# Sparse attention of the prompt: who weights and sums the index dots

## What is computed

```python
def indexer_scores(iq, iw, ik):
    dots = jax.nn.relu(jnp.einsum('bqhd,bsd->bqhs', iq, ik).astype(F32))
    return jnp.einsum('bqhs,bqh->bqs', dots, iw.astype(F32))

# for each block of 128 queries
sc = indexer_scores(iqb, iwb, ik)                 # 8 index heads
sc = jnp.where((key_pos[None, :] <= t[:, None])[None], sc, -jnp.inf)
_, idx = lax.top_k(sc, kk)                        # kk = 256
# softmax attention of 8 heads over the selected keys alone
```

## Time and profile before

| | us |
|---|---|
| median of 3 runs | 4081.56 (4080.29 to 4085.12) |
| the profiled execution | 4081.96 |
| its span, first to last instruction | 4079.6 |
| TensorE busy | 3440.1 (84%) |
| VectorE busy | 1736.2 (43%) |
| ScalarE busy | 1046.0 (26%) |
| GpSimd busy | 293.9 (7%) |

### The profile page before, as it was taken

How to read it: one execution, slowest core, us unless ns; L and a number is a source line. 1 busy time by engine, 2 the same in 40 slices (tenths; PEclk the granted TensorE clock), 3 DMA queues, 4 the chain that set the end, 5 groups by cost and what they waited for, 6 DMA issues and landing times. The chain is left out here.

```text
span 4079.6 us, 54190 instructions
## 1 busy us (share of the span) xinstructions
PE 3440.1 (84%) x20745; PEld 2868.6 (70%) x20771; DVE 1736.2 (43%) x2979; ACT 1046.0 (26%) x2049; POOL 293.9 (7%) x386
## 2 busy tenths in 40 slices
PE   8998849317568887889999999798599899999998
PEld 8986632105234444469999999797366699999997
DVE  2136611782378777521111256443244311112566
ACT  2134511001222222221111244321144311111444
POOL 0001122202000000000000000233000000000002
PEclk8997855558768877789999999898699899999999
DMA  3110122202300000011111211121200111112121
GB/s 98 43 41 21 31 73 58 62 6 63 118 16 19 19 18 11 11 50 43 46 41 46 89 40 51 43 46 64 79 29 27 47 46 41 46 41 80 51 59 45
DMA packets 235295, 189.81 MB, mean 47 GB/s; under 512 B 53473, under 2 KB 214258, under 8 KB 235090
## 3 DMA queue, kind: packets, MB, share of 16 engines
q1 hardware_dynamic: 227458, 169.84, 13.8%
q0 software_dynamic: 7664, 17.58, 1.4%
HBM read 158.11 MB, written 31.12 MB: 46 GB/s over the span
## 5 line engine op out<-in xcount | busy, mean ns | idle before, releaser
L1730 PE MATMUL ffn1u_ps<-h_hi,ffn1u_whi 128*128 128x384 f32 (+1 forms) x1056 | 348.1, 330 | 10.0 <-DVE h_lo L1792 10.0
L1730 PE MATMUL ffn0u_ps<-h_hi,ffn0u_whi 128*128 128x384 f32 (+1 forms) x1056 | 345.5, 327 | 9.0 <-DVE h_lo L1792 9.0
L1730 PE MATMUL ffn1u_ps<-h_hi,ffn1u_wlo 128*128 128x384 f32 (+1 forms) x1056 | 347.9, 329 | 0.0
L1730 PE MATMUL ffn1u_ps<-h_lo,ffn1u_whi 128*128 128x384 f32 (+1 forms) x1056 | 347.9, 329 | 0.0
L1730 PE MATMUL ffn0u_ps<-h_hi,ffn0u_wlo 128*128 128x384 f32 (+1 forms) x1056 | 345.5, 327 | 0.0
L1730 PE MATMUL ffn0u_ps<-h_lo,ffn0u_whi 128*128 128x384 f32 (+1 forms) x1056 | 345.3, 327 | 0.0
L157 PE MATMUL ine_ps<-ine_w_hi,ine_x_hi 128*128 128x256 f32 (+2 forms) x864 | 256.2, 297 | 1.3 <-DVE ine_w_lo L173 1.3
L157 PE MATMUL ine_ps<-ine_w_hi,ine_x_lo 128*128 128x256 f32 (+2 forms) x864 | 250.2, 290 | 0.0
L157 PE MATMUL ine_ps<-ine_w_lo,ine_x_hi 128*128 128x256 f32 (+2 forms) x864 | 249.7, 289 | 0.0
L1730 PEld LDWEIGHTS ffn1u_ps<-h_hi,ffn1u_whi 128*128 128x128 f32 x1056 | 198.9, 188 | 10.4 <-DVE ffn1u_wlo L1774 10.4
L1730 PEld LDWEIGHTS ffn0u_ps<-h_hi,ffn0u_whi 128*128 128x128 f32 x1056 | 199.2, 189 | 9.4 <-DVE ffn0u_wlo L1774 9.4
(11 more groups left out here) (413 smaller groups left out, 7556.9 us busy)
## 6 DMA issues: line engine op xcount, KB each, us to landing
ffn0u_raw<-in_ffn_w_gu_dram SPq DMA_DIRECT2D x44, 512.0 KB, 3.8
ffn1u_raw<-in_ffn_w_gu_dram SPq DMA_DIRECT2D x44, 512.0 KB, 3.8
ffn0d_w<-in_ffn_w_down_dram SPq DMA_DIRECT2D x88, 128.0 KB, 2.2
ffn1d_w<-in_ffn_w_down_dram SPq DMA_DIRECT2D x88, 128.0 KB, 2.2
ine_w<-in_w_in_even_dram SPq DMA_DIRECT2D x9, 1024.0 KB
smp_Kp<-in_cache_k_dram SPq DMA_DIRECT2D x128, 64.0 KB, 1.8
smp_Vp<-in_cache_v_dram POOLq DMA_DIRECT2D x96, 64.0 KB, 2.1
scratch_h<-ine_stage SPq DMA_DIRECT2D x20, 256.0 KB, 2.5
```

Of the source, the lines that this page charges most:

```text
L1730: last = nc.tensor.matmul(ps[:, t, k2, 0:n], wp[:, k2, k, :], hp[:, k, t0:t0 + n], start=(k == 0 and j == 0), stop=(k == KD - 1 and j == 2))
```

## The change

ScalarE gets a second pass over each relu'd dot, in place in rel: a Copy activation with the head's weight of each query as its scale. It waits for its own relu and, at a block's first dot, for the weights. GpSimd scales the weights, copies the pass of head 0 into sc and adds the others; for these it waits for dots_scaled and its own previous add, and at a block's first dot for search_begun, which VectorE now counts up after its first round , when sc has been read. The dots ahead of stage 0 stand in GpSimd's queue before the wait for the constants. The shift of a tile (L1181) now stands in the same queue: shift i - 1 ahead of stage i's dots. VectorE keeps the mask and the rounds. The ring of four, TensorE's order and the semaphore dots_added stay.

```diff
@@ ScalarE, bank7
                         nc.scalar.activation(rel[:, d % 4, 0:n], ps[:, dot_bank[u], 0:n], ACT.Relu).then_inc(dot_read, 1)
+                        if u[2:] == (0, 0):
+                            act.wait_ge(weighted, BLOCK.index(u[1]) - 1)
+                        act.wait_ge(dot_read, d + 1)
+                        nc.scalar.activation(rel[:, d % 4, 0:n], rel[:, d % 4, 0:n], ACT.Copy,
+                                             scale=iws[:, u[2]:u[2] + 1]).then_inc(dot_scaled, 1)
@@ GpSimd
-                pool.wait_ge(cin, 48)
-                for j in range(NO):
+                def add_dots(u):
+                    _, t, h, c = u
+                    d, n = dot_no[u], min(512, (t + 1) * P - 512 * c)
+                    if h == 0 and c == 0:
+                        if d == 0:
+                            pool.wait_ge(ki_in, 32)
+                        else:
+                            pool.wait_ge(dot_scaled, d)
+                        nc.gpsimd.tensor_scalar(iws[:, :], KI[:, t, kcol(C_IW):kcol(C_IW) + 8], IWS, None,
+                                                ALU.mult).then_inc(weighted, 1)
+                    part = sc[:, 512 * c:512 * c + n]
+                    pool.wait_ge(dot_scaled, d + 1)
+                    if h == 0:
+                        if d > 0 and c == 0:
+                            pool.wait_ge(search_begun, BLOCK.index(t) - 2)
+                        nc.gpsimd.tensor_copy(part, rel[:, d % 4, 0:n]).then_inc(dots_added, 1)
+                    else:
+                        pool.wait_ge(dots_added, d)
+                        nc.gpsimd.tensor_tensor(part, rel[:, d % 4, 0:n], part, ALU.add).then_inc(dots_added, 1)
+
+                def shift(j):
                     r = rows(out_tile[j])
                     pool.wait_ge(scaled, j + 1)
                     nc.gpsimd.tensor_tensor(X[0:r, j % RING_X, :], X[0:r, j % RING_X, :], gb[0:r, 1, :], ALU.add).then_inc(norm_done, 1)
+
+                for u in passes(-1):
+                    if u[0] == "dots":
+                        add_dots(u)
+                pool.wait_ge(cin, 48)
+                for i in range(NT):
+                    if i >= 1:
+                        shift(i - 1)
+                    for n in range(NH):
+                        for u in shares(i)[n][0]:
+                            if u[0] == "dots":
+                                add_dots(u)
+                for j in range(NT - 1, NO):
+                    shift(j)
@@ VectorE
-                def add_dots(u):
-                    _, t, h, c = u
-                    d, n = dot_no[u], min(512, (t + 1) * P - 512 * c)
-                    if h == 0 and c == 0:
-                        if d == 0:
-                            dve.wait_ge(ki_in, 32)
-                        link(nc.vector.tensor_scalar(iws[:, :], KI[:, t, kcol(C_IW):kcol(C_IW) + 8], IWS, None, ALU.mult))
-                    part = sc[:, 512 * c:512 * c + n]
-                    dve.wait_ge(dot_read, d + 1)
-                    if h == 0:
-                        nc.vector.tensor_scalar(part, rel[:, d % 4, 0:n], iws[:, h:h + 1], None, ALU.mult).then_inc(dots_added, 1)
-                    else:
-                        dve.wait_ge(dots_added, d)
-                        nc.vector.scalar_tensor_tensor(out=part, in0=rel[:, d % 4, 0:n], scalar=iws[:, h:h + 1], in1=part,
-                                                       op0=ALU.mult, op1=ALU.add).then_inc(dots_added, 1)
@@ VectorE, top_round
                     link(nc.vector.match_replace(wk[:, 0:L], m8[:, :], src[:, 0:L], TAKEN))
+                    if k == 0:
+                        dve.sem_inc(search_begun, 1)
@@ VectorE, order
-                for u in passes(-1):
-                    if u[0] == "dots":
-                        add_dots(u)
                         for u in share[n][0]:
-                            if u[0] == "dots":
-                                add_dots(u)
-                            elif u[0] == "out":
+                            if u[0] == "out":
                                 residual(u)
```

More of the change, by code:

```diff
@@ L881, in dsa_out @@
         dot_done, dot_read, dots_added = sem("dots_done"), sem("dots_read"), sem("dots_added")
-        b_done = sem("bias_ready")
+        b_done, weighted, search_begun, dot_scaled = sem("bias_ready"), sem("head_weights"), sem("search_begun"), sem("dots_scaled")
         s_done, m_done, e_done = sem("scores"), sem("max_done"), sem("probs")
```

## The result

The changed kernel takes 4039.0 us (median of 4, 4038.5 to 4040.5), the kernel before 4080.9 beside it: 0.9896 of it, 95% interval 0.9879 to 0.9913. Its profiled execution has a span of 4036.9 us against 4079.6. The page of its profile has busy time by engine, then VectorE's and GpSimd's slices.

A forecast was written before the change was run, and what follows sets the result against it. VectorE was taken to bound the sparse attention phase. Gains of 11.7 at the start and 4.9, 4.5, 7.5, 5.6, 5.9, 4.9 in stages 0 to 5 sum to 45.0 us: 4081.96 to 4037.0, with 8 in 10 for 4025 to 4062.

The forecast's parts named there:

- What bounds the phase, and what leaves VectorE: Sparse attention of the prompt: VectorE is the late engine; its removed work in stages 0 to 5 is 42.9 us.
- The start, 11.7: Ahead of stage 0: 16 dots run during the wait for constants, first row maximum at 1068.6; gain 11.7 us, bounds 7 and 13.
- Stage 0, 4.9: Full gain of 4.9 us: only four heads have dots, then TensorE's scores are there at +20.8 us, VectorE needs +21.2.
- Stage 1, 4.5: Two dots in each of four heads; scores of head 5 come 0.9 us after VectorE, so 4.5 of 5.5 us.
- Stages 2 and 3, 7.5 and 5.6: Four dots a head; TensorE's loops of 11.67 and 10.76 us cut the gain to 7.5 of 11.1 and 5.6 of 10.6.
- Stages 4 and 5, 5.9 and 4.9: Two dots a head; TensorE has room, so the gain is full, 5.9 and 4.9 us.
- GpSimd never needed, nothing else moved: Stages: GpSimd's 64 adds, about 71 us of 600, not needed until the next stage's first round; shift and store don't move.
- 1: Rival: GpSimd's adds hold VectorE up in stages 0 to 5; 71.4 us of adds, 4099 us, slower; chance 0.08.
- 2: Rival: relay through ScalarE dearer than its rows, 1.2 us for pass and wait; 4050 to 4054, tail to 4066; chance 0.22.
- 3: Rival: TensorE's loop does not hold VectorE back in stages 1 to 3; the whole 54.6 us, 4027; chance 0.10.
- 4: Rival: nothing moves, because heads are bound by TensorE throughout; 4078 to 4083 us; chance 0.05.
- The rule against the change: GpSimd's two-input add about twice as slow as VectorE's; by it the start's 16 dots would cost 10 us more.

The follow-up runs named there:

- e9: Changed kernel with the dots spread evenly over the heads in stages 0 to 3: 4023.24 us, 0.9860.
- e1: Kernel before, with VectorE's 16 dots ahead moved in front of its wait for the constants; VectorE still weights and adds all dots: 4065.95 us, 0.9961.
- e2: Changed kernel with GpSimd's wait for the constants put in front of its dots ahead of stage 0: 4054.99 us, 0.9938.
- e12: Changed kernel; in the stages ScalarE only takes the relu and GpSimd weights each dot itself before its add: 4035.0 us, 0.9891.
- e6: Changed kernel; in the stages ScalarE goes over each of the 64 weighted dots once more, a Copy by 1.0: 4041.13 us, 0.9905.
- e7: Changed kernel with half of TensorE's holding matmuls: 4071.7 us, 0.9942, in two groups (three executions at 4026 to 4049, five at 4070 to 4075).
- e5: Changed kernel; in the stages GpSimd does each of its 56 adds a second time, into an unread scratch tile: 4041.32 us, 0.9904.
- e4: Kernel before, with the 16 dots of stages 2 and 3 spread over all heads: 4075.48 us, 0.9987.
- e11: Kernel before, VectorE still weighting and adding all dots, with the order edits of e1 and e9: 4061.4 us, 0.9952.

## Why the prediction was right, and where its terms were off

The mechanism and the sign held, and 4037.0 lies 2 us from 4039.0. That closeness is partly luck: the terms of the phase summed to 45.0 and measured 39.6; the rest of the profiled difference is the spread behind the phase, and the median moved by 41.9.

- *What bounds the phase, and what leaves VectorE.* Right. e9 shows 41.3 us of the 42.9 once almost nothing else is late.
- *The start, 11.7.* 12.0 measured, of which 0.6 is that the constants landed earlier. The path was the one drawn: the constants come last, then the casts, the scores and the row maximum. I had left out that the two casts take 1.14 us beneath GpSimd's adds, where they had taken 0.36: the row maximum followed the constants by 2.6 us, 0.8 more than in e1. The earlier constants and shorter scores hid that in the sum. A relu and its weighting took 1.24 us, where I had 1.35 a dot and reckoned with 1.3, so the last relu ended at 1064.5 and not at 66.9, which moved nothing. Weighting 0.72 against my 0.73 and add 1.27 against 1.34 were right; the copy, taken at 1.0, took 0.61, and the adds ended at 1068.6 instead of 1070.3. That VectorE could have done it alone (e1) the prediction didn't say.
- *Stage 0, 4.9.* Mis-sized: 3.2. The step "four heads with dots, then TensorE's scores are there" took 6.56 us per TensorE loop plus ScalarE's pass. That loop had run at a granted clock of 0.76. In the changed kernel the transposes of heads 3 and 4 are 8.22 us apart, and the clock of the stretch is 0.57. The holding matmuls of 2.74 us are as long as before; the dots beside them take 3.4 us instead of 2.4:

```profile
1102.67 0.47 PE L1014 MATMUL dsa_ps<-ident,dsa_P 128*128 128x128 f32 x1
...
1104.65 2.74 PE L1044 MATMUL dsa_ps<-dsa_bias,dsa_identb 128*128 128x128 bf16 x24
...
1110.89 0.33 PE L1014 MATMUL dsa_ps<-ident,dsa_P 128*128 128x128 f32 x1 [0.38 <-ACT dsa_P L1122]
```

```profile
1100.00:1110.00 10.00, 9.53 (x39) 5.15 (x37) 9.72 (x14) 3.65 (x9) 1.50 (x2) 0.57 0.00 0
```

  In e2, with the same work a head, these transposes were 7.0 us apart at 0.76 and the stage gained its full 5.0. So I took the length of one loop at one clock as if it were fixed. That the relay is not the cause here e12 shows: without the second pass the loop took 8.42 us at 0.50. Why the clock stood lower in these heads no run shows.
- *Stage 1, 4.5.* Mis-sized: 3.5. TensorE's loop with the relay behind it cost 2.0 us of the 5.5 where I had 1.0. The passes themselves kept their price (relu, weighting, relu, weighting took 2.1 to 2.5 us against 2.4). Without the second pass (e12) the stage gains 5.5, with a third (e6) it gives back 3.6; but e7 keeps the relay, halves the holding matmuls and gains 5.3. Either one shortens the same loop, and the clock moved too (heads 3 and 4 at 0.65 and 0.75; e12 1.00), so how the missing 1.0 us divides between relay and clock stays open.
- *Stages 2 and 3, 7.5 and 5.6.* 6.0 and 4.0. The heads came at 11.67 and 10.75 us as forecast, row maxima 2 to 4 within 0.2 us. Then head 3 took 13.12 instead of 11.67: it carries the transposes of X (1.06 us on TensorE and a wait of 0.39). In the row of before the same gap was VectorE's and hid them; I had not priced them. These 1.5 us in each stage are the whole miss.

```profile
1266.02 1.06 PE L1037 MATMUL dsa_ps<-ident,dsa_X 128*128 128x128 f32 x8 [0.39 <-ACT dsa_PT L1133]
...
1277.66 1.09 PE L1014 MATMUL dsa_ps<-ident,dsa_P 128*128 128x128 f32 x8
```

- *Stages 4 and 5, 5.9 and 4.9.* 5.8 and 4.8.
- *GpSimd never needed, nothing else moved.* Right but for three relus of stage 5 that waited 1.10 us each for a place of the ring; the stage gave 4.8 of its 4.9 all the same. As to the rest, between the stages all is within 0.5 us, but for 1.2 us more at the start of stage 5, where TensorE ran at 0.50 from 1516 to 1524.
- *Rivals.* 1 fell in the stages (e5); at the start GpSimd's adds cost VectorE's casts 0.8 us. 2 fell as it was put: pass and wait took 0.64 us (1.24 less a relu of 0.60) and not 1.2. The relay is on the path in stage 1 and at the start of e2 at its usual price. 3 fell for the changed kernel and nearly holds for e9. 4 fell.
- *The rule against the change.* GpSimd's add of 512 columns took 1.27 us and VectorE's multiply-add 0.75, 1.7 times. The Trainium skill (GPSIMD Engine Reference, Engine selection) has two-input operations about twice as slow there, and the trace agrees roughly. It cost nothing in time, since GpSimd was not last.

## What to carry to other kernels

Work taken off the bounding engine pays only up to the next engine's own loop: measure that loop head by head, with everything a particular head carries, and at the clock that it then runs at, which you know only from the profile after. After such a move look at the schedule again: spreading the work that had been bunched gave 15.8 us more, and filling the freed engine's waits at the start of each stage 34 more. And try first what order alone gives: one wait moved behind work that didn't need it was worth 12 of the 42 us. Last, compare profiles stage by stage: two executions can differ by 3.3 us in a stage that the edit doesn't touch.

## What the runs showed of the hardware

- GpSimd's multiply by a per-query weight is dear: 1.57 us for 512 columns with one input, against 1.27 for an add of two and 0.61 for a copy. ScalarE did the same multiply in 0.72. The Trainium skill (GPSIMD Engine Reference, Engine selection) has one-input operations at roughly line rate; this form is not (605 ns at 128 columns and 1566 at 512, so 2.5 ns a column; the copy 292 and 610, 0.8 a column).
- ScalarE's pass cost 722 ns with the weight read from SBUF and 630 with a constant (e6). The Trainium skill (ScalarE: Activation LUTs, What ACT_TABLE_LOAD costs) gives 93 ns for such an operand; the trace agrees.
- GpSimd's adds slow VectorE's casts, not its search. The two bias casts took 0.36 us together with GpSimd idle (before, e1, e2, e4, e11) and 1.14 to 1.32 beneath its adds (the other eight profiles); 56 more adds left max and match-replace at 1.223 and 1.209. The Trainium skill (SBUF — State Buffer, Who interferes with whom) draws that line: an operation with at most one SBUF input contends with GpSimd only in a two-port mode, which a cast can enter; the trace agrees.
- TensorE's clock can outweigh the work: half the holding matmuls of a head in stage 2 are 1.5 us of work at the upper level; without them the head ran at 0.50 and took 7.3 us longer in the profiled execution of e7, while in stages 0 and 1 leaving them out saved 1.7 and 1.8 us. What else would hold the clock was not tried.
